# Causal attention heads: the copy of the last block's transposed weights moves ahead of the next head's rotation transfers in ScalarE's program

## The reference, cut to what matters

```python
q = apply_rope(rmsnorm(q.reshape(b, S, H, 2, D), q_norm_w), cos, sin)
k = apply_rope(rmsnorm(k.reshape(b, S, H, 2, D), k_norm_w), cos, sin)
...
def one_block(args):                      # 4 blocks of 128 queries, 4 heads
    s = jnp.einsum("bqhcd,bkhcd->bhcqk", q_blk, k) * scale
    p = jax.nn.softmax(jnp.where(mask, s, -jnp.inf), axis=-1)
    w = p[:, :, 0] - lam * p[:, :, 1]
    return jnp.einsum("bhqk,bkhe->bqhe", w.astype(v.dtype), v)
...
o = rmsnorm(o, subln_w) * (1.0 - lambda_init)
```

## Time and profile before

| | us |
|---|---|
| median of 3 runs | 3044.29 (3043.07 to 3045.87) |
| the profiled execution, its own time | 3046.89 |
| its span in the trace | 3045.3 |
| TensorE busy | 2964.5 (97%) |
| ScalarE busy | 971.5 (32%) |

### The profile page before, as it was taken

The page is one execution under the profiler, slowest core; times in us unless marked ns, Lnnn a source line. Parts: engine busy times, 40 slices in busy tenths (PEclk is TensorE's granted clock), DMA queues, the critical chain, the costliest instruction groups (busy, mean ns, idle before and its releaser), DMA issues.

```text
span 3045.3 us, 39268 instructions
## 1 busy us (share of the span) xinstructions
PE 2964.5 (97%) x15124; PEld 2343.0 (77%) x15124; DVE 1797.5 (59%) x2354; ACT 971.5 (32%) x1679; POOL 2006.9 (66%) x1885
## 2 busy tenths in 40 slices
PE   8999999999999999999999999999999999899998
PEld 5887777688878878777888677777777777688886
DVE  8645887761474559777417533334888888910513
ACT  5343123330234331333203223233544455411411
POOL 6765676578756656756768555556576777666765
PEclk9999999999999999999999999999999999999999
DMA  4222222234323222222433222222222222142322
GB/s 172 98 104 100 88 91 87 72 140 134 124 78 107 102 93 89 93 79 77 175 125 109 75 79 79 71 86 70 77 82 70 83 84 81 46 159 97 111 85 109
DMA packets 59962, 295.50 MB, mean 97 GB/s; under 512 B 6880, under 2 KB 7264, under 8 KB 30592
## 3 DMA queue, kind: packets, MB, share of 16 engines
q1 hardware_dynamic: 40880, 253.77, 24.3%
q10 hardware_dynamic: 18896, 39.22, 3.7%
HBM read 275.08 MB, written 12.65 MB: 94 GB/s over the span
## 4 chain that ended last, share of the span: by engine, by line
PE 84%; DVE 10%; ACT 3%; POOL 1%; issue 1%; ACTq 0%; DVEq 0%; DMA 0%; SPq 0%; POOLq 0%
PE bank L441 69%; PE bank L965 5%; PE bank L775 1%; PE bank L792 1%; ACT att_sc L1330 1%; PE bank L784 1%; PE bank L868 1%; PE bank L957 1%; PE bank L843 1%; DVE att_sc L2175 1%; DVE h_lo L1819 1%; POOL w_lo L2625 1%; PE bank L861 1%; DVE h_lo L1847 1%; DVE att_sc L2187 0%
## 5 line engine op out<-in xcount | busy, mean ns | idle before, releaser
L441 PE MATMUL bank<-h_hi,w_lo 128*128 128x512 f32 x3456 | 1391.5, 403 | 26.0 <-POOL w_lo L2625 15.4
L2625 POOL TENSOR_TENSOR w_lo<-w_raw,w_hi 128x512 fp32r<-128x512 f32 x936 | 1310.0, 1400 | 78.1
L441 PE MATMUL bank<-h_hi,w_hi 128*128 128x512 f32 x3456 | 1352.2, 391 | 0.0
L441 PE MATMUL bank<-h_lo,w_hi 128*128 128x512 f32 x3456 | 1350.4, 391 | 0.0
L2623 POOL TENSOR_SCALAR w_hi<-w_raw 128x512 fp32r<-128x512 f32 x936 | 717.5, 767 | 933.8 <-PE bank L441 705.5
L441 PEld LDWEIGHTS bank<-h_hi,w_lo 128*128 128x128 f32 x3456 | 651.7, 189 | 215.7 <-issue 55.1
L441 PEld LDWEIGHTS bank<-h_hi,w_hi 128*128 128x128 f32 x3456 | 651.2, 188 | 139.7
L441 PEld LDWEIGHTS bank<-h_lo,w_hi 128*128 128x128 f32 x3456 | 652.4, 189 | 135.4 <-issue 8.4
L1033 ACT ACTIVATE raw<-bank 128x512 f32<-128x512 f32 x148 | 88.6, 599 | 384.1 <-PE bank L441 345.6
L2100 DVE SCALAR_TENSOR_TENSOR bank<-cfm_up,par,bank 128x512 f32<-128x512 f32 x232 | 175.4, 756 | 8.3
L1799 DVE TENSOR_TENSOR sumsq<-sumsq,bank 128x512 f32<-128x512 f32 x64 | 44.0, 688 | 172.3 <-ACT bank L1726 145.4
(11 more groups left out here) (375 smaller groups left out, 2971.5 us busy)
## 6 DMA issues: line engine op xcount, KB each, us to landing
w_raw<-in_wall SPq DMA_DIRECT2D x224, 1024.0 KB, 4.9
w_raw<-in_wall SPq DMA_DIRECT2D x40, 256.0 KB, 3.4
ssd_abc<-acs_scratch ACTq DMA_DIRECT2D x16, 512.0 KB, 5.3
x_scratch<-xT ACTq DMA_DIRECT2D x8, 1024.0 KB, 8.2
xT<-x_scratch ACTq DMA_DIRECT2D x8, 1024.0 KB, 11.0
xT<-in_x ACTq DMA_DIRECT2D x4, 1024.0 KB, 12.2
xT<-in_x SPq DMA_DIRECT2D x3, 1024.0 KB, 10.9
out<-last_z SPq DMA_DIRECT2D x3, 1024.0 KB, 3.9
```

What stands on the lines that cost most here:

```text
L441: mm = t.matmul(bank[BANK[u]][:, :], w[:, CS16[k]], h[:, k, :], start=(k == 0 and w is m.w_lo[b]), stop=(k == KT - 1 and w is m.w_hi[b] an ...
L2625: g.tensor_tensor(m.w_lo[b][:, part], m.w_raw[b][:, part], m.w_hi[b][:, part].bitcast(F32), ALU.subtract).then_inc(*s.lo.inc(u, n))
```

## The change

In the loop over heads 0 to 2 of both layers, ScalarE's `turn(h, 3)` (wait for TensorE's transposes of block 3, then the copy to att_wT) stands ahead of the q transfers and of the copy of unit v, where it stood behind both.

```diff
             scores(h, 3)
             turn(h, 2)
             roots(l, h + 1)
+            turn(h, 3)
             swap(l, h + 1, 0)
             evac(u1, m.raw[2])
-            turn(h, 3)
             swap(l, h + 1, 1)
             output(h)
```

## The result

| | us |
|---|---|
| before, median of 19 runs | 3045.17 (3042.36 to 3048.70) |
| changed, median of 19 runs | 3050.75 (3047.49 to 3053.73) |
| ratio, changed to before | 1.0015, 95% interval 1.0009 to 1.0022 |
| the profiled execution after, its own time and its span | 3049.60, 3048.0 |

The change makes the kernel slower by 0.15%, about 4.6 us, and 2.7 to 6.7 us by the interval (the medians lie 5.6 us apart). The ratio is under the bound of 0.2% that the prediction set, but its interval reaches just over it. The forecast was 3047.2 (+0.1%).

A forecast was written before the change was run, and what follows sets the result against it. TensorE, with 84% of the chain, was taken as the bound. Terms summed to -0.1 + 0 + 3.0 = +2.9 us, giving 3047.2 us (+0.1%) against the timed median of 3044.29; range 3041.7 to 3052.0.

The forecast's parts named there:

- Term 1: At the product with the values, TensorE's wait for the att_wT copy goes: 9.8 us over six places.
- Term 2: At `finish`, the wait for ScalarE's square grows and gives the gain back; -0.1 us for terms 1 and 2 together.
- Term 3: On ScalarE in head 0, q transfers and copy of v come later; cost 0, 0.5 us at most.
- Term 4: Behind four longer gaps at `finish`, TensorE's clock falls to half in two of four, 1.5 us each: +3.0 us.
- The rival with all four falling: Half clock behind `finish` in heads 1 and 2 of both layers, 1.7 us each: 3051.0, +0.22%; chance 0.13.
- the one with one to three: Main case: the wait moves to `finish` and one to three stretches at half clock come; chance 0.62.
- The rival in which TensorE keeps its gain: TensorE keeps the 9.8 us gained at the product: 3034.5, -0.32%; chance 0.05.
- The rival with late q transfers: In head 0, swapped q lands too late for VectorE, at most 1.1 us in two heads: 3046.4; chance 0.04.

The follow-up runs named there:

- e4: Changed kernel with ScalarE's square and copy of the head's output moved ahead of the k transfers; ratio to before 0.9998.
- e5: Kernel before, att_wT copy in its old place, with ScalarE's square and copy of the output moved ahead of the k transfers; ratio to before 0.9991.
- e1: Kernel before with the att_wT copy's new place in head 0 of each layer only, heads 1 and 2 in the old order; ratio to before 1.0000.
- e3: Changed kernel with 12 extra unread 128x512 matmuls ahead of `finish` in heads 1 and 2; ratio to before 0.9997.
- e2: Kernel before with the att_wT copy's new place in heads 1 and 2 only, head 0 as before; ratio to before 1.0016.
- e12: Kernel before with 8 extra unread 128x512 matmuls ahead of the product in heads 1 and 2; ratio to before 0.9998.
- e11: e5 with 8 extra unread 128x512 matmuls ahead of the product in heads 1 and 2; ratio to before 0.9983.
- e6: Changed kernel with one of the two quarters behind `finish` moved ahead of it in heads 1 and 2; ratio to before 1.0021.

## Why the prediction was right

*Term 1, the product's wait goes.* Right in all six places.

*Term 2, it comes back at `finish`.* Right: 14.5 us against a forecast of about 13, and the start of `finish` against att_uk unchanged (3.23 us, 3.24 before). The gap is 3.17 us and not 2.87, because the 2.05 us in the row of before understates what TensorE could gain: without a wait the product took 1.05 us instead of 1.16, and began 0.2 us earlier against `finish` than I had put it. That the square's place behind the k transfers makes the wait is shown by e4 and e5.

*Term 3, what ScalarE does later.* The cost of 0 was right, as e1 shows, and the working was too cautious. ScalarE at the end of head 0, after:

```profile
499.10 0.60 ACT L1337 ACTIVATE att_wT<-bank 128x512 f32<-128x512 f32 x1 [2.79 <-PE bank L663]
499.11 2.44 ACTq L1307 DMA_DIRECT2D att_tq<-att_uq  x4
501.65 0.60 ACT L1033 ACTIVATE raw<-bank 128x512 f32<-128x512 f32 x1 [1.95 <-issue]
503.20 2.44 ACTq L1307 DMA_DIRECT2D att_tk<-att_uk  x4
```

The q transfers are issued beside the copy, 0.01 us behind its start, and not behind its end. They move by 0.5 us and not by 1.1.

*Term 4, the clock.* The direction and the mechanism were right: e3 shows that the clock is the loss. The size was taken too low in the number of falls and about right in their price. I took two of four at 1.5 us; the profile shows four, at 1.43 us, and 7 of 8 with e2. With four the sum would have been 3044.29 - 0.1 + 5.7 = 3049.9; by the ratio the loss is 4.6 us.

The trace of the kernel before spoke for more than two of four. It holds six gaps over 2.1 us between TensorE's matmuls, of which I read two, and the clock fell behind or within each. The other four:

```profile
73.48 0.47 PE L441 MATMUL bank<-h_hi,w_lo 128*128 128x512 f32 x1 [2.89 <-POOL w_lo L2625]
1685.31 0.80 PE L441 MATMUL bank<-h_hi,w_lo 128*128 128x512 f32 x1 [5.04 <-DVE h_lo L1819]
2656.43 0.50 PE L441 MATMUL bank<-h_hi,w_lo 128*128 128x512 f32 x1 [2.20 <-DVE h_lo L1819]
3015.77 0.50 PE L965 MATMUL bank<-w_lo,h_hi 128*128 128x512 f32 x1 [2.29 <-POOL w_lo L2625]
```

The rival with all four falling used 1.7 us each and came to +0.22%. That price is half of a 3.4 us stretch. By the matmuls' starts each stretch in fact put TensorE back by 1.5 to 1.6 us, and up to 0.3 us of it came back before the next `finish`. The reason I gave for a lower price, a stretch that begins inside the gap, holds for one of the four, and there for under 0.2 us: the clock falls between 603.05 and 603.06 us, `finish` starts at 603.23.

The measured loss (4.6 us by the ratio, 5.6 by the medians) thus lies between the forecast's 2.9 and the rival's 6.7. The range holds it because it was drawn wide enough for both cases, and not because the count was right: in the profiled execution it was the case with all four falls that came, to which I gave 0.13, and not the one with one to three, to which I gave 0.62. The loss over the 19 runs, 4.6 us, is smaller than the 5.7 us of that execution; how many of the four fall in the other executions no trace shows. That the kernel before may hold such a stretch too is supported by e1, in heads that keep the old order (no profile of the kernel before shows it in these heads), and its effect is too small for e12 to show.

*The rival in which TensorE keeps its gain* was wrong for the reason given. Its number, 3034.5, would not even have come with `finish` free: e4 shows VectorE, and then the clock, as the next limits.

*The rival with late q transfers* did not come: VectorE's first use of the swapped q starts at 508.35 after and 508.22 before, the 0.13 us of the whole trace. Its sum was also misprinted by 0.2 us: 1.1 us in two heads is 2.2, which gives the 3046.4 that stands there.

## What to carry to other kernels

A wait that is taken away moves to the next point at which the same engines meet, unless what makes that point late moves too; read the chain through it before counting the gain. Two short gaps of the bound engine joined to one long gap can be worse than both apart, though their sum is nearly the same: here the clock fell more often behind the long one (7 of 8 against 6 of 12), and no later wait absorbed the loss. Where a gap cannot be filled with needed work without delaying something else, matmuls without a use can pay: 12 of them at each of four places took back the loss of 0.15% (e3), and eight at each of four places went with the one clear gain (e11, 0.9983 where e5 without them has 0.9991; the two intervals overlap, but the falls are gone and each layer is 3.1 us shorter). To forecast the number of falls, list all gaps of that length in the trace of before and count: here it was six of six, where the forecast took half.

## What the runs showed of the hardware

- The same kernel's gap of 2.05 us was followed by a stretch at clock 0.50 in some places and not in others (e1, layers 0 and 1), and of gaps of 3.17 us one in e2 was not. Over the whole span, the clock fell at all six gaps over 2.1 us in the profile of before and at eight of ten in that of the changed kernel; the gap of 2.29 us near the end of the third layer is in both, with a fall behind it in the first and none in the second. In the changed kernel such a stretch lasted 3.4 us (6 x 0.28 / 0.5) and cost 1.43 us behind `finish`, counted to the last `finish` of the layer.
- Matmuls that do nothing but run held the clock: with 0.45 us of idle time or less ahead of `finish` instead of 3.17 it stayed at 1.00 in all four places of e3.
- ScalarE's queue issued transfers while the copy ahead of them still ran (issue from 499.11, copy from 499.10 for 0.60 us).
- VectorE's 128x512 step L1790 took 0.69 us while GpSimd was idle and 1.57 beside GpSimd's weight splitting (e6, at all four places where the quarter was moved). There the order that started GpSimd earlier made VectorE slower at the place where TensorE then waited for it.
